# Every second weight load of the experts issued by GpSimd's queue

## The chip, the cores and the metric

The kernel runs on one core of a Trainium2 chip. The metric is the device time of one execution in microseconds. TensorE multiplies, ScalarE and VectorE prepare operands and empty the accumulators, GpSimd does small vector work and can issue DMAs, SyncE only issues DMAs. All DMAs run on the core's 16 DMA engines, whoever issues them.

## What is computed

Four transformer layers on x of shape (1, 256, 1024) in float32: two of a first block, two of a second. The last layer ends in a mixture of eight experts, and this is where the change lies (the rest cut):

```
def swiglu(x, w13, w2):
    a, g = jnp.split(x @ w13, 2, axis=-1)
    return (jax.nn.silu(a) * g) @ w2

def moe_ffn(x, router_w, router_b, w13, w2):
    logits = x @ router_w + router_b
    top_v, top_i = lax.top_k(logits, 2)
    wts = jax.nn.softmax(top_v, axis=-1)
    gate = jnp.einsum('bsk,bske->bse', wts, jax.nn.one_hot(top_i, 8))
    y = jnp.zeros_like(x)
    for e in range(8):
        y = y + gate[..., e:e + 1] * swiglu(x, w13[e], w2[e])
    return y
```

w13 of an expert is 1024 x 7168, w2 is 3584 x 1024. All eight experts' weights, 352 MB, are read once; a layer norm follows.

## The kernel before

**Slots.** All weights lie in memory as a stream of slots, [128 partitions, 2048 words], 1 MB each; this document counts the experts' slots from 0. An expert has 42: 28 for the hidden layer (seven chunks of 512 columns, four slots each) and 14 for the down projection. So the experts have slots 0 to 335. `Stream` plans for each slot where it lands (`place`), which slot held that buffer before (`before`) and which count of the buffer's semaphore tells of its landing (`turn`). From slot 2 on the ring is four buffers used once, then raw0 to raw2 and spare0, spare1 in turn, so that a buffer comes round every five slots.

**What happens to a slot.** Matmuls run as three products of float32 halves. A slot is loaded by `s_slot`, SyncE's DMA at L2595, when the rest of the slot before it in the buffer has been taken (`lo`). ScalarE copies it, in two halves of 1024 columns, to the rounded part wh (L1163, `a_hi`), in one of three sets, for which TensorE must have finished the slot three earlier (`freed`). VectorE takes the rest, wl = raw - wh, also in two halves (L1617, `v_lo`). This read is the last of the raw buffer. TensorE multiplies wh and wl with the tokens (L480 to L482).

**Experts.** Tokens are gathered per expert by products with a selection, 128 at most (GH, GL). After each chunk come an activation (TT, TU), a transpose (L710) and a split (EH, EL). The result of experts 0 to 6 goes to Y (L1172, ScalarE) and from there, by GpSimd's DMA at L2562 in `g_parts`, to a part of scratch_parts in memory. At the end GpSimd issues four indirect DMAs (L2568) that gather each token's rows of the parts into CHOICE[0] to CHOICE[3], once expert 7's last hidden chunk is multiplied. VectorE adds them to X (L2376, `v_add_choice`): its order, written out by hand, puts one addition behind the rest of slot 330, one behind that of 331, of 332 and of 333. Expert 7's own result goes by YH and YL through a product into X (L2330), then the norm and the stores to out.

**Order.** Each engine runs its instructions in the order in which they are written, and a wait holds all behind it. SyncE's queue holds the loads of all slots in order. GpSimd's holds its small vector work up to the last norm but one, then the seven stores and the four gathers, and then the last norm's two roots. The lines for the heavy case (more than 128 tokens for an expert) are compiled and not run here.

Of the kernel before, what the change touches and what calls it, by code (L numbers as in the profile page):

```python
# [243 lines left out]
    return EXPERTS + EXPERT * e  # L244


class Stream:


    def __init__(self):  # L250
        plan = [s for f in (layer_one_slots, layer_two_slots) for l in range(2) for s in f(l)]
        plan += [s for e in range(8) for s in expert_slots(e)]
        self.words = [slot_words(s) for s in plan]
        self.split = [s != "mlstm" for s in plan]
        self.half = [sum(r1 - r0 for _, _, r0, r1, _, _ in s[:1]) // 2 if s != "mlstm" else 0 for s in plan]
        self.source, at = [], 0
        for s, n in enumerate(self.words):
            if s == expert_slot(8):
                at = self.source[expert_slot(0)]
            self.source.append(at)  # L260
            at += 128 * n
        self.number, c = [], 0
        for split in self.split:
            self.number.append(c)
            c += split
        ring = ["raw0", "raw1", "raw2"]
        more, once, spare = ["more0", "more1"], ["once0", "once1", "once2", "once3"], ["spare0", "spare1"]
        into = {BASE[0] + MIX + 3: more, BASE[1] + MIX + 3: more, BASE[2] + BR + 3: more}
        self.place, self.before, self.turn = [], [], []
        held, turns = {}, {}  # L270
        for s in range(len(plan)):
            if s in into:
                ring = more + ring
            if s in (BASE[1] + 2, BASE[2] + 2, BASE[3] + 2):
                ring = [r for r in ring if r not in more]
            if s == EXPERTS + 2:
                ring = once + ring + spare
            r = ring.pop(0)
            if r not in once:
                ring.append(r)  # L280
            self.place.append(r)
            self.before.append(held.get(r))
            turns[r] = turns.get(r, 0) + (s > 0)
            self.turn.append(turns[r])
            held[r] = s


def program(nc, x_d, pos_d, ws_d, vec_d, row_d, ln_d, rel_d, relb_d, rw_d, cst_d, one_d, lnc_d, out_d):
# [6 lines left out]
    stream = Stream()  # L295
    ctx = ExitStack()
    with ctx:
# [134 lines left out]
            signals.append(Signal(ctx.enter_context(nc.semaphore("s_" + name)), step))  # L432
            return signals[-1]

        landed = {n: ctx.enter_context(nc.semaphore("s_" + n)) for n in raws}
        x_in, cst_in, small_in = [signal(f"x{t}_in", 16) for t in range(2)], signal("cst_in", 16), signal("small_in", 16)
        ident_in, zeroed = signal("ident_in", 16), signal("zeroed")
        first_half, second_half = signal("first_half", 16), signal("second_half", 16)
# [712 lines left out]
        def a_hi(s):  # L1151

            while a_at[0] <= min(s, until[0]):
# [2 lines left out]
                if not stream.split[n]:  # L1156
                    continue
                half = stream.words[n] // 2
                A.wait_ge(landed[stream.place[n]], 16 * stream.turn[n])
                if c >= NSET:  # L1160
                    A.wait_ge(*freed[c - NSET])
                for i in range(2):
# [1393 lines left out]

        def g_parts():

            for e in range(7):
                for h in range(2):  # L2560
                    G.wait_ge(*out("dn", ("e", e), 0, h))
                G.q.dma_start(parts[128 * e:128 * e + 128, :], Y[e % 2][:, :]).then_inc(*part_out[e % 2].mark(e))  # L2562
            G.wait_ge(*picked.at())
            for x in (5, 6):
                G.wait_ge(*part_out[x % 2].at(x))
            G.wait_ge(*full("gu", ("e", 7), 6, 0))
            for i in range(4):
                G.q.indirect_dma_start(  # L2568
                    out=CHOICE[i][:, :], out_offset=None, in_=parts,
                    in_offset=bass.IndirectOffsetOnAxis(ap=ROWS[:, i:i + 1], axis=0),  # L2570
                    bounds_check=7 * 128 - 1, oob_is_err=False).then_inc(*choice_in[i].mark())

        def s_slot(n):

# [23 lines left out]
        def sync_front():  # L2598
# [15 lines left out]
            S.q.dma_start(PT[0:32, 384:392], rel_d).then_inc(*small_in.mark())  # L2614
            S.q.dma_start(PT[0:8, 512:896], lnc_d).then_inc(*small_in.mark())
            for n in range(3, expert_slot(8)):
                s_slot(n)
                if n == BASE[1] + HID + 4:
                    S.wait_ge(*scr_out.at())
                    S.wait_ge(*out("sc", 1, "b", 1, 3))  # L2620
# [118 lines left out]
```

## Time and profile before

| | us |
|---|---|
| median of 3 runs | 2260.6 (2260.22 to 2260.81) |
| the profiled execution | 2262.25 |
| its span | 2261.0 |
| TensorE busy in it | 2241.1 (99%) |
| VectorE busy | 1733.3 (77%) |
| ScalarE busy | 1370.5 (61%) |
| GpSimd busy | 83.6 (4%) |

The experts run from about 1290 us to the end. The DMA engines move 568.75 MB for SyncE's queue in all, 5.77 MB for GpSimd's (the software queue, q0) and 9.52 MB for ScalarE's (q10). A SyncE queue's row is written SPq, and L2595 is line 2595 of the kernel. A matmul's recorded duration overlaps the next one's, so TensorE's busy time doesn't show how fast it goes; the steps of the engines that wait for it do.

### The profile page before, as it was taken

What the parts mean: (1) busy time and instruction counts of PE and PEld (TensorE: products, weight loads), DVE (VectorE), ACT (ScalarE), POOL (GpSimd) and SP (SyncE); (2) the same over time, 40 slices, a digit from 0 to 9 for tenths busy, and PEclk for the clock granted to TensorE, in tenths of its full rate; (3) what the DMA queues carried; (4) which work ended last, traced back from release to release, by engine and by line L of the source; (5) the groups of instructions that cost most, each with busy time, mean ns of one, the idle gap of its engine ahead of it and who ended that gap; (6) DMA issues with size and microseconds to landing.
All of it is one profiled execution on the core that took longest, in us unless ns stands there. A gap on an engine that the chain in (4) does not pass through costs nothing.

```text
span 2261.0 us, 30455 instructions
## 1 busy us (share of the span) xinstructions
PE 2241.1 (99%) x12336; PEld 1926.5 (85%) x12336; DVE 1733.3 (77%) x2226; ACT 1370.5 (61%) x1794; POOL 83.6 (4%) x106
## 2 busy tenths in 40 slices
PE   9999999999999999999999999999999999999997
PEld 6998888898888999888899888888888888888886
DVE  6976556877554578655678898989998899989898
ACT  5654444655443454444454587777777777777775
POOL 2200001300000000000100000000000000000001
PEclk9999999999999999999999999999999999999999
DMA  7455453545544435555434599999999999999996
GB/s 260 161 185 193 176 200 145 178 169 214 188 182 149 179 131 210 189 199 189 151 107 170 225 360 383 378 357 376 379 385 362 364 376 389 366 362 374 386 373 245
DMA packets 95891, 586.05 MB, mean 259 GB/s; under 512 B 21968, under 2 KB 23296, under 8 KB 26624
## 3 DMA queue, kind: packets, MB, share of 16 engines
q1 hardware_dynamic: 80496, 568.75, 66.9%
q10 hardware_dynamic: 13664, 9.52, 1.5%
q0 software_dynamic: 1584, 5.77, 0.6%
q8 instruction: 99, 1.62, 0.3%
q14 instruction: 48, 0.39, 0.0%
HBM read 579.27 MB, written 4.73 MB: 258 GB/s over the span
## 4 chain that ended last, share of the span: by engine, by line
PE 95%; DVE 2%; issue 1%; ACT 1%; DMA 1%; POOL 0%; ACTq 0%; DVEq 0%
PE bank L480 28%; PE bank L482 28%; PE bank L481 28%; PE bank L477 9%; PE bank L710 2%; PE bank L756 1%; DVE wl L1617 1%; PE bank L510 1%; DMA raw<-in_ws 1%; POOL SM L2469 0%; PE bank L804 0%; ACT wh L1163 0%; DVE BIAS L1963 0%; DVE X L2330 0%; DVE X L2376 0%
## 5 line engine op out<-in xcount | busy, mean ns | idle before, releaser
L1617 DVE TENSOR_TENSOR wl<-raw,wh 128x1024 fp32r<-128x1024 f32 x698 | 820.1, 1223 | 229.1 <-ACT wh L1163 225.7
L1163 ACT ACTIVATE wh<-raw 128x1024 fp32r<-128x1024 f32 x704 | 704.5, 1054 | 305.5 <-PE bank L482 264.6
L480 PE MATMUL bank<-wh,GH 128*128 128x512 f32 x896 | 352.7, 394 | 0.0
L482 PE MATMUL bank<-wh,GL 128*128 128x512 f32 x896 | 349.3, 390 | 0.0
L481 PE MATMUL bank<-wl,GH 128*128 128x512 f32 x896 | 348.9, 389 | 0.0
L1617 DVE TENSOR_TENSOR wl<-spare,wh 128x1024 fp32r<-128x1024 f32 x264 | 310.0, 1221 | 30.4 <-ACT wh L1163 28.0
L1163 ACT ACTIVATE wh<-spare 128x1024 fp32r<-128x1024 f32 x264 | 264.2, 1054 | 58.9 <-PE bank L482 56.8
L480 PE MATMUL bank<-HH,wh 128*128 128x256 f32 x832 | 239.6, 288 | 0.0
L481 PE MATMUL bank<-HL,wh 128*128 128x256 f32 x832 | 235.3, 283 | 0.0
L482 PE MATMUL bank<-HH,wl 128*128 128x256 f32 x832 | 235.3, 283 | 0.0
L480 PE MATMUL bank<-wh,HH 128*128 128x512 f32 (+1 forms) x600 | 224.9, 375 | 2.5 <-DVE wl L1617 2.3
L482 PE MATMUL bank<-wh,HL 128*128 128x512 f32 (+1 forms) x600 | 223.4, 372 | 0.0
L481 PE MATMUL bank<-wl,HH 128*128 128x512 f32 (+1 forms) x600 | 223.3, 372 | 0.0
L482 PEld LDWEIGHTS bank<-wh,GL 128*128 128x128 f32 x896 | 168.2, 188 | 35.6
L481 PEld LDWEIGHTS bank<-wl,GH 128*128 128x128 f32 x896 | 168.4, 188 | 33.9
L480 PEld LDWEIGHTS bank<-wh,GH 128*128 128x128 f32 x896 | 168.3, 188 | 33.6
L480 PE MATMUL bank<-wh,EH 128*128 128x512 f32 x448 | 176.4, 394 | 0.5 <-DVE wl L1617 0.4
L481 PE MATMUL bank<-wl,EH 128*128 128x512 f32 x448 | 174.7, 390 | 0.0
L482 PE MATMUL bank<-wh,EL 128*128 128x512 f32 x448 | 174.5, 390 | 0.0
L1617 DVE TENSOR_TENSOR wl<-more,wh 128x1024 fp32r<-128x1024 f32 x94 | 111.0, 1222 | 73.0 <-ACT wh L1163 72.8
L480 PEld LDWEIGHTS bank<-HH,wh 128*128 128x128 f32 x832 | 159.3, 192 | 3.5 <-issue 3.0
L481 PEld LDWEIGHTS bank<-HL,wh 128*128 128x128 f32 x832 | 159.5, 192 | 0.2
(295 smaller groups left out, 3420.7 us busy)
## 6 DMA issues: line engine op xcount, KB each, us to landing
raw<-in_ws SPq DMA_DIRECT2D x352, 1024.0 KB, 6.3
spare<-in_ws SPq DMA_DIRECT2D x132, 1024.0 KB, 7.0
more<-in_ws SPq DMA_DIRECT2D x48, 1024.0 KB, 4.8
once<-in_ws SPq DMA_DIRECT2D x4, 1024.0 KB, 12.0
scratch_parts<-Y POOLq DMA_DIRECT2D x7, 512.0 KB, 8.4
REL<-in_relb ACTq DMA_DIRECT2D x4, 768.0 KB, 12.8
LNB<-in_ln ACTq DMA_DIRECT2D x3, 1024.0 KB, 5.8
LNB<-in_ln ACTq DMA_DIRECT2D x4, 512.0 KB, 4.3
```

Of the source, the lines that this page charges most:

```text
L477: return T.q.matmul(o, l, r, start=start, stop=stop)
L480: T.q.matmul(o, l[0], r[0], start=start, stop=False)
L481: T.q.matmul(o, l[0], r[1], start=False, stop=False)
L482: return T.q.matmul(o, l[1], r[0], start=False, stop=stop)
L510: ins = T.q.transpose(room[:, 128 * c:128 * c + 128], src[:, a:a + 128], ident)
L710: ins = T.q.transpose(room[:, 128 * k:128 * k + 128], TU[t][:, 128 * k:128 * k + 128], ident)
L756: ins = T.q.transpose(room[:, 128 * n:128 * n + 128], LB[t][:, 256 * h + 128 * i:256 * h + 128 * i + 128], ident)
L1163: A.q.activation(sets[c % NSET][0][:, half * i:half * i + half], raws[stream.place[n]][:, half * i:half * i + half], ACT.Copy).then_inc(*h ...
L1617: V.q.tensor_tensor(wl[:, half * i:half * i + half], raw[:, half * i:half * i + half], wh[:, half * i:half * i + half].bitcast(f32), ALU.s ...
```

## The change

Slots of odd number from 9 to 335 are issued by GpSimd, through its own DMA queue, in place of SyncE. They keep their buffers, and they wait for the same rest of the slot before. Since the two queues' landings in one buffer can't share a semaphore's count, the landings by GpSimd have semaphores of their own (`lands`), and ScalarE waits for the one that belongs to the slot.

```
+def by_pool(s):
+    return EXPERTS + 8 < s < expert_slot(8) and (s - EXPERTS) % 2 == 1
...
+            own = r + "_pool" if by_pool(s) else r
+            turns[own] = turns.get(own, 0) + (s > 0)
+            self.turn.append(turns[own])
+            self.lands.append(own)
...
-                A.wait_ge(landed[stream.place[n]], 16 * stream.turn[n])
+                A.wait_ge(landed[stream.lands[n]], 16 * stream.turn[n])
...
+            n = expert_slot(0) + 9
             for e in range(7):
+                while n < expert_slot(e + 1) + 6:
+                    g_slot(n)
+                    n += 2
                 for h in range(2):
                     G.wait_ge(*out("dn", ("e", e), 0, h))
                 G.q.dma_start(parts[128 * e:128 * e + 128, :], Y[e % 2][:, :]).then_inc(*part_out[e % 2].mark(e))
+            while n < expert_slot(8):
+                g_slot(n)
+                n += 2
             G.wait_ge(*picked.at())
...
+        def g_slot(n):
+
+            r = stream.place[n]
+            if stream.before[n] is not None:
+                G.wait_ge(*lo.at(stream.before[n], 1))
+            if r.startswith("spare"):
+                G.wait_ge(*full("rt", 1))
+            words = stream.words[n]
+            G.q.dma_start(raws[r][:, 0:words], bass.AP(ws_d.tensor, stream.source[n], [[words, 128], [1, words]])
+                          ).then_inc(landed[stream.lands[n]], 16)
...
             for n in range(3, expert_slot(8)):
-                s_slot(n)
+                if not by_pool(n):
+                    s_slot(n)
```

The GpSimd queue at the end of the program, before: the last two stores of parts and, next to them, the four gathers (L2562 is the store, L2568 the gather).

```order
84 L2562 DMA scratch_parts<-Y_78 128x1024 [waits s_out7,s_out6]
85 L2562 DMA scratch_parts<-Y_77 128x1024 [waits s_out1,s_out0]
86 L2568 DMA CHOICE_79<-scratch_parts,ROWS 128x1024 [waits s_part0_out,s_full5,s_part1_out,s_picked]
87 L2568 DMA CHOICE_80<-scratch_parts,ROWS 128x1024
88 L2568 DMA CHOICE_81<-scratch_parts,ROWS 128x1024
89 L2568 DMA CHOICE_82<-scratch_parts,ROWS 128x1024
```

The same place now (L2594 is `g_slot`, L2581 the gather; the last row of a slot is slot 335 in spare1):

```order
214 L2594 DMA raw<-in_ws 128x2048 [waits s_lo]
215 L2594 DMA spare_87<-in_ws 128x2048 [waits s_lo]
216 L2594 DMA raw<-in_ws 128x2048 [waits s_lo] x2
217 L2594 DMA spare_89<-in_ws 128x2048 [waits s_lo]
218 L2581 DMA CHOICE_79<-scratch_parts,ROWS 128x1024 [waits s_part0_out,s_full5,s_part1_out,s_picked]
219 L2581 DMA CHOICE_80<-scratch_parts,ROWS 128x1024
220 L2581 DMA CHOICE_81<-scratch_parts,ROWS 128x1024
221 L2581 DMA CHOICE_82<-scratch_parts,ROWS 128x1024
```

Between the last store and the first gather there now stand the loads of expert 7 from its slot 7 on, up to slot 335, which waits for the rest of slot 330.

VectorE's order at the end, the same before and after (L1617 takes the rest of a slot, both halves; L2376 adds a gathered tile; row 1403 is slot 330, row 1412 slot 335):

```order
1403 L1617 TENSOR_TENSOR wl<-spare_89,wh 128x1024 [waits s_hi] x2
1404 L2376 SCALAR_TENSOR_TENSOR X<-CHOICE_79,PICK,X 128x1024 [waits s_choice_weight,s_scaled,s_choice0_in]
1405 L1617 TENSOR_TENSOR wl<-raw,wh 128x1024 [waits s_hi] x2
1406 L2376 SCALAR_TENSOR_TENSOR X<-CHOICE_80,PICK,X 128x1024 [waits s_choice1_in]
1407 L1617 TENSOR_TENSOR wl<-raw,wh 128x1024 [waits s_hi] x2
1408 L2376 SCALAR_TENSOR_TENSOR X<-CHOICE_81,PICK,X 128x1024 [waits s_added,s_choice2_in]
1409 L1617 TENSOR_TENSOR wl<-raw,wh 128x1024 [waits s_hi] x2
1410 L2376 SCALAR_TENSOR_TENSOR X<-CHOICE_82,PICK,X 128x1024 [waits s_added,s_choice3_in]
1411 L1617 TENSOR_TENSOR wl<-spare_87,wh 128x1024 [waits s_hi] x2
1412 L1617 TENSOR_TENSOR wl<-spare_89,wh 128x1024 [waits s_hi] x2
```

Nothing moved here; what moved is the gather that row 1404 waits for, behind the load that waits for row 1403.

## Rows read from the trace of the kernel before

**Rows 1.** Windows (busy us of each engine, count, clock, DMA share, GB/s): body of experts.
```profile
1300.00:2205.00 905.00, 905.00 (x4140) 750.46 (x4138) 818.25 (x784) 707.92 (x787) 4.03 (x7) 1.00 0.97 373
```
**Rows 2.** Waits from 1300 to 2200 us (total, times, longest), engines and SyncE's queue.
```profile
ACT wh L1163 <- PE bank L482: 140.8, 212, 1.0
...
SPq L2595 <- DVE wl L1617: 794.0, 314, 13.6
```
**Rows 3.** Landing of the spare slots' 125 DMAs, 1300 to 2200 us.
```profile
DMA to landing us min/median/max: 4.7/7.0/9.2
```
**Rows 4.** Timeline (start, us): SyncE's loads of slots 2 to 5 and 43, ScalarE's split of 43.
```profile
1280.10 2.03 SPq L2595 DMA_DIRECT2D once<-in_ws  x4
...
1397.44 0.33 SPq L2595 DMA_DIRECT2D raw<-in_ws  x1
...
1407.57 2.01 ACT L1163 ACTIVATE wh<-raw 128x1024 fp32r<-128x1024 f32 x2 [0.71 <-PE bank L482]
```
**Rows 5.** Line L1617 (ns min/median/max): 1300 to 2205 us, then 1411.4 to 1416.
```profile
L1617 DVE TENSOR_TENSOR wl<-raw,wh x382: 1215/1219/1228, 1305.7 to 2203.6; 128x1024 fp32r<-128x1024 f32 x191
...
L1617 DVE TENSOR_TENSOR wl<-spare,wh x4: 1219/1222/1227, 1411.8 to 1415.2; 128x1024 fp32r<-128x1024 f32 x4
```
**Rows 6.** Timeline of the end: ScalarE's splits of 328 to 330, VectorE from 330 on.
```profile
2218.69 2.01 ACT L1163 ACTIVATE wh<-raw 128x1024 fp32r<-128x1024 f32 x2 [0.71 <-PE bank L482]
2221.41 2.01 ACT L1163 ACTIVATE wh<-spare 128x1024 fp32r<-128x1024 f32 x2 [0.71 <-PE bank L482]
2224.75 2.01 ACT L1163 ACTIVATE wh<-spare 128x1024 fp32r<-128x1024 f32 x2 [1.33 <-DMA spare<-in_ws]
...
2225.85 2.36 DVE L1617 TENSOR_TENSOR wl<-spare,wh 128x1024 fp32r<-128x1024 f32 x2 [0.98 <-ACT wh L1163]
2228.13 1.28 DVE L2376 SCALAR_TENSOR_TENSOR X<-CHOICE,PICK,X 128x1024 f32<-128x1024 f32 x1
...
2238.73 1.28 DVE L2376 SCALAR_TENSOR_TENSOR X<-CHOICE,PICK,X 128x1024 f32<-128x1024 f32 x1
```
**Rows 7.** Chain that ended last, a piece of it (start, us).
```profile
2231.88 1.06 DVE X L2376
```
**Rows 8.** DMA view: windows 1280.4 to 1281.2, 1411.4 to 1415.7, 1415.7 to 1418.5, 2207.7 to 2212.
```profile
GB/s 0 0 0 0 0 0 0 0 0 0 0 0 0 0 0 0 0 0 0 0 0 0 0 0 0 0 0 0 0 0 0 0 410 0 0 819 819 0 0 0
...
DMA packets 186, 1.39 MB, mean 324 GB/s; under 512 B 16, under 2 KB 16, under 8 KB 16
...
q1 hardware_dynamic: 186, 1.39, 101.0%
...
q0 software_dynamic: 144, 0.52, 45.8%
...
q1 hardware_dynamic: 230, 1.66, 94.7%
```
**Rows 9.** GpSimd's DMAs: timeline of first store, first and last gather; landings of gathers, stores.
```profile
1411.42 0.80 POOL L2562 DMA_DIRECT2D scratch_parts<-Y  x1 [133.23 <-ACT Y L1172]
...
2207.70 1.09 POOL L2568 DMA_INDIRECT CHOICE<-scratch_parts,ROWS  x1 [77.82 <-PE bank L482]
...
2211.70 0.99 POOL L2568 DMA_INDIRECT CHOICE<-scratch_parts,ROWS  x1 [0.30 <-issue]
...
DMA to landing us min/median/max: 8.6/12.7/16.9
...
DMA to landing us min/median/max: 6.7/8.4/9.3
```
**Rows 10.** Windows around the first store, and after the last one's issue.
```profile
1409.90:1412.90 3.00, 3.00 (x15) 2.49 (x14) 2.21 (x2) 2.65 (x4) 0.80 (x1) 1.00 1.04 399
1412.90:1415.90 3.00, 3.00 (x15) 2.48 (x14) 3.00 (x4) 2.19 (x3) 0.00 (x0) 1.00 0.92 279
...
1418.00:1426.00 8.00, 8.00 (x37) 6.64 (x36) 7.64 (x10) 6.51 (x7) 0.00 (x0) 1.00 1.01 424
...
2130.90:2133.90 3.00, 3.00 (x14) 2.47 (x14) 3.00 (x4) 2.20 (x3) 0.00 (x0) 1.00 0.97 255
```

More of the change, by code:

```diff
@@ L268, in __init__ @@
         into = {BASE[0] + MIX + 3: more, BASE[1] + MIX + 3: more, BASE[2] + BR + 3: more}
-        self.place, self.before, self.turn = [], [], []
+        self.place, self.before, self.turn, self.lands = [], [], [], []
         held, turns = {}, {}
@@ L282, in __init__ @@
             self.before.append(held.get(r))
-            turns[r] = turns.get(r, 0) + (s > 0)
-            self.turn.append(turns[r])
+            own = r + "_pool" if by_pool(s) else r
+            turns[own] = turns.get(own, 0) + (s > 0)
+            self.turn.append(turns[own])
+            self.lands.append(own)
             held[r] = s
@@ L433, in signal @@
             return signals[-1]
-        landed = {n: ctx.enter_context(nc.semaphore("s_" + n)) for n in raws}
+        landed = {n: ctx.enter_context(nc.semaphore("s_" + n)) for n in sorted(set(stream.lands))}
         x_in, cst_in, small_in = [signal(f"x{t}_in", 16) for t in range(2)], signal("cst_in", 16), signal("small_in", 16)
```

## The prediction, made before the changed kernel was run

> **What bounds the kernel now.** I read the windowed busy times first. From 1300 to 2205 us, TensorE is busy in all 905 us at a granted clock of 1.00 (the 2.4 GHz level), VectorE in 818 and ScalarE in 708, and the DMA engines move 373 GB/s at a busy share of 0.97 [rows 1]. The waits of that stretch name no engine waiting for a DMA: ScalarE waits 141 us for TensorE to give back a split set, and SyncE's queue waits 794 us for VectorE to free a raw buffer [rows 2]. So in the body of the experts the weights arrive early, the matmuls set the pace, and SyncE spends its time waiting, not issuing: an issue lasts 0.33 us [rows 4]. Nothing is to be won by sharing its issuing.
>
> How early do they arrive? A landing takes 4.7 to 9.2 us, median 7.0 [rows 3]. Slot 43 is issued at 1397.44 and ScalarE begins to split it at 1407.57 [rows 4], 10.1 us later, so 3.1 us lie between the median landing and its use. Behind that stands a second cover. ScalarE may start on a slot when TensorE has finished the one three earlier; two slots of 2.72 us (2218.69 to 2221.41 [rows 6]) then remain, 5.4 us, and the new slot needs about 2.3 (half a split 1.05, half a rest 1.22 [rows 5]). That leaves 3.1 us more: TensorE starves when a landing takes longer than about 13.2 us.
>
> The end is different. From slot 330 on VectorE is the path: rests of slots and four additions of the gathered tiles alternate, and the chain of waits runs through them [rows 6, 7].
>
> **Part 1: SyncE issues 164 slots fewer** (9, 11, ... 335). 164 x 0.33 us lie inside its 794 us of waiting. Slots that stay on SyncE wait for the same rest as before; only the neighbours' places in the queue go. Worth 0.
>
> **Part 2: each of these slots starts later.** A DMA of SyncE on an idle queue shows its first packet 1.0 us after its issue (issued 1280.10, the first bytes fall in the 33rd of 40 slices of the 0.8 us from 1280.4, at 1281.1 [rows 4, 8]). A DMA of GpSimd is slower to begin: the store of a part is issued at 1411.42, there is no packet of the software queue by 1415.7, and all 144 come by 1418.5; the gathers issued from 2207.70 have none by 2212.0 [rows 8, 9]. I take 4.4 us, so 3.4 more than SyncE. A GpSimd slot would land after 8.1 to 12.6 us, median 10.4. The longest is still under 13.2. The two queues share the 16 engines, which adds up to one transfer (1 MB at 424 GB/s [rows 10], 2.5 us) to a landing that meets another; but about 2 us of waiting behind a neighbour are already in the median of 7.0, since an unhindered landing takes 4.7. The lateness doesn't add up either: the slot that follows in the same buffer is five further, so it is SyncE's, with 3 us to spare. I take 0 for the body. The cover that hides it is 3.1 + 3.1 us; if it is gone, the next part's rival B says what it costs.
>
> The Trainium skill (DMA: Bandwidth & Descriptors, Specifications) gives a first byte after about 1 us for GpSimd's path and 0.6 for SyncE's. This trace disagrees for GpSimd (4.4), and I go by the trace.
>
> **Part 3: does VectorE suffer?** At 818 of 905 us it has little to spare, so blocked instructions would matter. The four rests that run from the store's issue at 1411.42 to 1416 take 1219 to 1227 ns, as the 382 rests of slots in raw do over the whole body (1215 to 1228) [rows 5]. 0 us.
>
> **Part 4: GpSimd's own queue.** Two kinds of DMA stand in it. The seven stores of parts are needed only by the gathers and two experts later: free, even if a slot in front holds them. Slot 7 of the next expert stands behind each store, which waits for the Y copy; it waits itself for the rest of a slot that TensorE must first make room for, after expert 0's last product, and the Y copy waits for no more than that product. 0 us.
>
> The four gathers of the end are not free. Before, they are issued from 2207.70, as soon as expert 7's last hidden chunk is multiplied. Now slots up to 335 come first, and 335 waits for the rest of slot 330, which ends at 2225.85 + 2.36 = 2228.2 [rows 6]. On VectorE the first addition stands right behind that rest, and behind the addition the rests of 331 to 335, for which TensorE waits. Step by step:
> - Rest of 330: before, its split waited 1.33 us for a DMA that competed with the gathers [rows 6]. Without them it starts one step of 2.72 after 2221.41, at 2224.1, 0.6 earlier: rest ends 2227.6.
> - Issue of slot 335 (0.5 to 0.8, as of a store [rows 9]) and 0.3 between issues: first gather issued 2228.4.
> - Its landing took 8.6 us before (least of the four [rows 9]): 2237.0. Lower bound 6.7 us, the fastest store of the same size [rows 9]: 2235.1. Upper bound: slot 335's 1 MB is ahead in the same queue, 2.5 us more, 2239.5; and if the four landings spread as before (last issued about 4.0 after the first, landing 16.9 after its issue: 2249.3 against the fourth addition's 2238.73 [rows 6, 9]), +10.6.
> - The first addition ran at 2228.13; now at 2237.0: **+8.9 us**, with +7.0 and +13 as ends (11.4, and the spread on top). From there VectorE's chain repeats in its old steps of 3.5 us, against gathers that come some 3.7 apart, so I add 0.5.
> TensorE can't cover this: it has slots 329 and 330 left, some 5 us, and the five slots after them need VectorE. What follows slot 335 (YH, YL, the scatter, the norm, the stores, 16.5 us) is unchanged and moves along.
>
> **Sum.** The profiled execution took 2262.25 us (span 2261.0), 1.65 above the median of 2260.6. 2262.25 + 0 + 0 + 0 + 9.4 = 2271.6 for it, and **2270.0 us** as a median: 0.4% slower. Own range of this case 2266 to 2275.
>
> **Rival B: the DMA engines become the bound in the body.** In all seven cases the weight stream is slow from 1.5 to 4.5 us after a GpSimd store is issued, before its first packet moves: 279 GB/s at the first and 255 at the last, against 399 in the 3 us ahead of the first and 424 after it [rows 10]. If a weight DMA of GpSimd does this too, it costs 3 x (424 - 279) / 424 = 1.0 us of the engines' time. A pair of slots then needs 2 x 2.47 + 1.03 = 5.97 us. TensorE's pair takes 5.68: 373 GB/s over 905 us less 3.7 MB of stores are 318 slots, 2.84 each. 0.29 x 164 = 47 us, and the tail: **2317 us**, up to 2330 where down-projection pairs (5.44) are not averaged with the others. For it: seven of seven. Against it: the gathers, also GpSimd's, show no such dip (1.66 MB in the 4.3 us from 2207.7, 386 GB/s [rows 8]), so it may belong to stores. It decides from 0.74 us of lost time per DMA on.
>
> **Rival C: landings over 13 us now and then**, where a store lies between two slots (three GpSimd DMAs in 6 us, seven times) or where slots queue in pairs: 1 to 3 us each, 2275 to 2290.
>
> **Rival D, not slower: the gather lands in time.** The 4.4 us may be the cost of waking an idle GpSimd (the first store came after 133 us of idleness [rows 9]) and not of each DMA. If a busy one starts in SyncE's 1.0 us, the first gather has its 0.5 MB by 2228.4 + 1.0 + 1.3 + 0.4 = 2231.1, +3.0 us, 2263.6. It decides below 4.2 us from issue to landing (2232.6, 4.5 us after 2228.13). This is also what the skill's first byte of 1 us, cited above, would make of the tail.
>
> **How the numbers follow.** Tail alone 0.50 (2270); B 0.30 (2295 to 2335); C 0.12; D 0.08, of which 0.02 goes below 2256. The range 2263 to 2320 leaves out the rest of D (about 0.05) and the upper half of B (about 0.13). This kernel's runs can tell about 0.2% (4.5 us) from no change. Faster by more than that 0.02, within it 0.06, slower 0.92.
>
> **What would show it.** Right: in 1300 to 2205 TensorE busy throughout and no wait for a DMA; software-queue landings near 10 us; the gathers issued at about 2228; VectorE idle for some 9 us before the first addition, released by the gather; everything behind it 9 us later. B: TensorE with gaps all through the body, splits waiting for DMAs, a busy share near 1 at less than 373 GB/s. C: such gaps only at the stores. D: gathers that land within 4 us. I would be wrong altogether if the gathers were issued before slot 335, or if VectorE's rests grew beyond 1.23 us.

## The result, and the profile after

The changed kernel takes 2269.61 us (median of 6 runs, 2268.45 to 2271.45), the kernel before 2260.55 beside it (6 runs, 2260.13 to 2261.05). The ratio is 1.0039, 95% interval 1.0029 to 1.005: 9.1 us slower. Its profiled execution took 2268.45 us with a span of 2267.2, 6.2 us more than the one of before (2262.25; span 2261.0); it is the fastest of the six.

The program gained six lines, so each line of before has a higher number now: the splits are L1169, the rests L1623, the additions L2382, the products L486 to L488. GpSimd's stores are L2572, its gathers L2581, its weight loads L2594; SyncE's loads are L2619.

First the page of the changed kernel: the queues (packets, MB, share of the 16 engines' span) and the DMA issues (KB each, median us to landing).

```profile
q1 hardware_dynamic: 56880, 396.78, 47.0%
q0 software_dynamic: 25200, 177.74, 20.2%
...
raw<-in_ws POOLq DMA_DIRECT2D x98, 1024.0 KB, 7.8
spare<-in_ws POOLq DMA_DIRECT2D x66, 1024.0 KB, 7.8
```

So the change does what it says: 98 + 66 = 164 loads go through the software queue, and they land 7.8 us after their issue, not the 10.4 that I had forecast. The same two groups read over the body, 1300 to 2200 us, GpSimd's loads first and SyncE's second, against 4.7/7.0/9.2 in [rows 3]:

```profile
DMA to landing us min/median/max: 4.9/7.8/12.4
...
DMA to landing us min/median/max: 4.8/7.9/10.8
```

Both queues are later by about 0.9 us in the median, SyncE's too, and GpSimd's has the longer tail. Did it cost anything? The windowed busy times of the body (columns as in [rows 1]), and the waits of 1300 to 2200 us (total, times, longest):

```profile
1300.00:2205.00 905.00, 904.98 (x4137) 750.13 (x4136) 817.01 (x784) 707.33 (x787) 89.35 (x166) 1.00 0.96 373
```

```profile
ACT wh L1169 <- PE bank L488: 123.9, 188, 1.0
...
ACT wh L1169 <- DMA raw<-in_ws: 12.7, 10, 2.7
...
ACT wh L1169 <- DMA spare<-in_ws: 7.8, 6, 3.0
```

No: ScalarE now waits 16 times for a weight, 20.5 us in all (14 of the 16 for a load of GpSimd), where the list of before had no such wait, and its wait for TensorE shrinks by 17 us in exchange [rows 2]. TensorE stays busy in 904.98 of 905 us at a granted clock of 1.00. The late landings are absorbed by slack that ScalarE had: of the 315 landings of both queues, 12 took over 10.1 us, the time from issue to use that [rows 4] gave.

The end is where the time went. The timelines of ScalarE, VectorE and GpSimd there (start us, us, then in brackets the idle time before and its releaser), to be laid beside [rows 6, 9]:

```profile
2217.35 2.01 ACT L1169 ACTIVATE wh<-raw 128x1024 fp32r<-128x1024 f32 x2 [0.71 <-PE bank L488]
...
2223.89 2.36 DVE L1623 TENSOR_TENSOR wl<-spare,wh 128x1024 fp32r<-128x1024 f32 x2 [0.36 <-ACT wh L1169]
2234.54 1.28 DVE L2382 SCALAR_TENSOR_TENSOR X<-CHOICE,PICK,X 128x1024 f32<-128x1024 f32 x1 [8.29 <-DMA CHOICE<-scratch_parts,ROWS]
...
2244.94 1.28 DVE L2382 SCALAR_TENSOR_TENSOR X<-CHOICE,PICK,X 128x1024 f32<-128x1024 f32 x1
...
2226.54 0.54 POOL L2594 DMA_DIRECT2D spare<-in_ws  x1 [4.90 <-DVE wl L1623]
2227.50 1.08 POOL L2581 DMA_INDIRECT CHOICE<-scratch_parts,ROWS  x1 [0.42 <-issue]
```

Read from the bottom: slot 335 is issued at 2226.54, after a wait for the rest of slot 330; the first gather follows at 2227.50, and VectorE stands idle for 8.29 us until it has landed at 2234.5. In the waits of 2205 to 2267 us the products appear behind it:

```profile
DVE X L2382 <- DMA CHOICE<-scratch_parts,ROWS: 8.3, 1, 8.3
PEld bank L486 <- DVE wl L1623: 6.8, 2, 6.6
PE bank L486 <- DVE wl L1623: 6.2, 1, 6.2
```

TensorE had no such gap before. One step more is in the windows from 2229 us on:

```profile
2229.00:2232.00 3.00, 1.86 (x9) 1.20 (x7) 0.00 (x0) 2.29 (x4) 2.39 (x3) 1.00 0.96 400
2232.00:2236.00 4.00, 0.00 (x0) 0.00 (x0) 1.46 (x2) 0.95 (x2) 0.48 (x1) 0.85 1.01 412
2236.00:2240.00 4.00, 2.99 (x7) 2.41 (x8) 4.00 (x4) 0.00 (x0) 0.00 (x0) 0.50 0.27 112
2240.00:2245.00 5.00, 5.00 (x20) 4.03 (x20) 5.00 (x6) 2.02 (x3) 0.00 (x0) 0.83 0.00 0
```

TensorE has no product from 2230.9 to 2237.0; its granted clock falls in that time, stands at 0.50, the 1.2 GHz level, from 2236 to 2240, and is back to 1.00 in the window from 2245 us. That costs nothing here, since VectorE sets the pace: from the first addition to the end of the span are 32.7 us (2267.2 - 2234.54), and they were 32.9 before (2261.0 - 2228.13).

The two profiled executions are not at the same place when the end begins: slot 328 is split at 2217.35 here and at 2218.69 there [rows 6]. Measured from that split, the first addition comes after 17.19 us, and came after 9.44: **+7.75 us** for the end in the traces. The lead is older than the body: the first split of the experts' slots already starts at 1290.78 after and at 1292.59 before. It is no sign of the change either: in the five traces of kernels that are the same as the one before up to there, this split starts anywhere from 1291.09 to 1293.06, and in the four with shared loads from 1290.78 to 1292.51. One of the first splits of the body, in spare, starts at 1341.41 in the timeline after and at 1343.07 in the one before. From it to the split of 328 are 875.94 us after and 875.62 before: the body costs **+0.3 us** in this one execution (the run below with the same shared loads in the body has 875.65). 7.75 + 0.32 - 1.66 of lead - 0.21 behind the first addition are the 6.2 us between the two spans.

### The profile page after: what moved, and what is told of

It is laid out like the page before. It is cut to its first block, busy times and chain, and to the rows that moved or that the text cites. A ratio compares the mean times of both kernels' runs of the same rounds, so it can differ in the third digit from the quotient of the medians.

```text
span 2267.2 us, 30455 instructions
## 1 busy us (share of the span) xinstructions
PE 2241.7 (99%) x12336; PEld 1926.1 (85%) x12336; DVE 1731.6 (76%) x2226; ACT 1369.8 (60%) x1794; POOL 172.7 (8%) x270
## 4 chain that ended last, share of the span: by engine, by line
PE 95%; DVE 2%; DMA 1%; issue 1%; ACT 0%; POOL 0%; ACTq 0%; SPq 0%; DVEq 0%; POOLq 0%
PE bank L486 28%; PE bank L488 28%; PE bank L487 28%; PE bank L483 8%; PE bank L716 2%; PE bank L762 1%; DVE wl L1623 1%; PE bank L516 1%; DMA raw<-in_ws 0%; POOL SM L2475 0%; DMA CHOICE<-scratch_parts,ROWS 0%; ACT wh L1169 0%; PE bank L810 0%; ACTq L1358 0%; DVE BIAS L1969 0%
## 5 line engine op out<-in xcount | busy, mean ns | idle before, releaser
L1623 DVE TENSOR_TENSOR wl<-raw,wh 128x1024 fp32r<-128x1024 f32 x698 | 819.8, 1222 | 229.0 <-ACT wh L1169 226.2
L1169 ACT ACTIVATE wh<-raw 128x1024 fp32r<-128x1024 f32 x704 | 704.2, 1053 | 306.9 <-PE bank L488 255.5
L486 PE MATMUL bank<-wh,GH 128*128 128x512 f32 x896 | 352.9, 394 | 0.0
L488 PE MATMUL bank<-wh,GL 128*128 128x512 f32 x896 | 349.3, 390 | 0.0
L1623 DVE TENSOR_TENSOR wl<-spare,wh 128x1024 fp32r<-128x1024 f32 x264 | 309.8, 1220 | 31.9 <-ACT wh L1169 30.5
L1169 ACT ACTIVATE wh<-spare 128x1024 fp32r<-128x1024 f32 x264 | 264.1, 1054 | 69.2 <-PE bank L488 61.3
L486 PE MATMUL bank<-HH,wh 128*128 128x256 f32 x832 | 239.6, 288 | 0.0
L488 PE MATMUL bank<-HH,wl 128*128 128x256 f32 x832 | 235.2, 283 | 0.0
L486 PE MATMUL bank<-wh,HH 128*128 128x512 f32 (+1 forms) x600 | 224.9, 375 | 1.6 <-DVE wl L1623 1.6
L488 PE MATMUL bank<-wh,HL 128*128 128x512 f32 (+1 forms) x600 | 223.4, 372 | 0.0
L488 PEld LDWEIGHTS bank<-wh,GL 128*128 128x128 f32 x896 | 168.2, 188 | 35.6
L486 PEld LDWEIGHTS bank<-wh,GH 128*128 128x128 f32 x896 | 168.3, 188 | 34.3 <-DVE wl L1623 0.4
L486 PE MATMUL bank<-wh,EH 128*128 128x512 f32 x448 | 177.4, 396 | 6.2 <-DVE wl L1623 6.2
L488 PE MATMUL bank<-wh,EL 128*128 128x512 f32 x448 | 175.3, 391 | 0.0
L1623 DVE TENSOR_TENSOR wl<-more,wh 128x1024 fp32r<-128x1024 f32 x94 | 111.0, 1222 | 73.1 <-ACT wh L1169 72.9
L486 PEld LDWEIGHTS bank<-HH,wh 128*128 128x128 f32 x832 | 159.3, 191 | 3.5 <-issue 3.0
## 6 DMA issues: line engine op xcount, KB each, us to landing
once<-in_ws SPq DMA_DIRECT2D x4, 1024.0 KB, 13.2
```

The lines of the kernel that those rows point to most:

```text
L486: T.q.matmul(o, l[0], r[0], start=start, stop=False)
L488: return T.q.matmul(o, l[1], r[0], start=False, stop=stop)
L1169: A.q.activation(sets[c % NSET][0][:, half * i:half * i + half], raws[stream.place[n]][:, half * i:half * i + half], ACT.Copy).then_inc(*h ...
L1623: V.q.tensor_tensor(wl[:, half * i:half * i + half], raw[:, half * i:half * i + half], wh[:, half * i:half * i + half].bitcast(f32), ALU.s ...
```

## The experiments

Four concern the end of the program, two the body, three take one buffer away to see what the body's cover is worth, and the last tries to shorten the end. All were run with the kernel before on the same chip: its medians were 2260.78 (24 runs, for the experiments on the kernel before with waiting gathers, the gathers ahead of the last loads, and GpSimd alone), 2260.91 (27, for the last four slots back on SyncE, ScalarE's stores, and the first two with four buffers) and 2260.93 (15, for the last two). They differ from the kernel before or from the changed one, as the text above each diff says.

### The changed kernel with the last four slots back on SyncE

From the changed kernel; slots 329, 331, 333 and 335 leave GpSimd's queue.

```diff
 def by_pool(s):
-    return EXPERTS + 8 < s < expert_slot(8) and (s - EXPERTS) % 2 == 1
+    return EXPERTS + 8 < s < expert_slot(8) - 8 and (s - EXPERTS) % 2 == 1
...
-            while n < expert_slot(8):
+            while n < expert_slot(8) - 8:
                 g_slot(n)
```

> The changed kernel with slots 329, 331, 333 and 335 given back to SyncE; GpSimd issues the 160 loads 9 to 327 and then the gathers, at their old time. Nothing of the weights is ahead of the gathers on GpSimd's queue, and nothing behind them. Theory (the loss comes from gathers and last loads sharing one queue, in either order): 2260.8 us, within 1.0. Rival (some loss belongs to the loads of the body): 2262 to 2266.

Measured: 2261.32 us (11 runs, 2260.53 to 2262.28), ratio 1.0001 (0.9992 to 1.001). GpSimd's last load, its first gather, and VectorE's first addition in the timelines:

```profile
2205.24 0.54 POOL L2594 DMA_DIRECT2D raw<-in_ws  x1 [4.02 <-DVE wl L1623]
2207.78 1.09 POOL L2581 DMA_INDIRECT CHOICE<-scratch_parts,ROWS  x1 [2.00 <-PE bank L488]
...
2227.90 1.28 DVE L2382 SCALAR_TENSOR_TENSOR X<-CHOICE,PICK,X 128x1024 f32<-128x1024 f32 x1
```

The gathers are issued at the old time again, the addition waits for nothing, and the loss is gone, with 160 of the 164 loads still on GpSimd. Its body has the landings of the changed kernel (8.0 us for SyncE's, 7.9 for GpSimd's) and TensorE busy in all 905.00 us. So the whole measurable loss hangs on the four last loads, and none on the other 160.

### The kernel before with gathers that wait for the rest of slot 330

From the kernel before: the wait of slot 335 is given to the gathers, and no load is moved.

```diff
             G.wait_ge(*full("gu", ("e", 7), 6, 0))
+            G.wait_ge(*lo.at(expert_slot(8) - 6, 1))
             for i in range(4):
```

> The kernel before, all loads by SyncE, but GpSimd waits for the rest of slot 330 before it issues the gathers. Theory: the same wait as in the changed kernel, less the 1.0 us that the issue of slot 335 took there ahead of the gathers: first gather issued about 2227.7, landed 7.0 later, 2268.0 to 2269.0 us. Rival (the loads are the cost): 2260.6.

Measured: 2268.7 us (5 runs, 2267.91 to 2269.71), ratio 1.0036 (1.0022 to 1.005). Gather and addition:

```profile
2227.24 1.09 POOL L2569 DMA_INDIRECT CHOICE<-scratch_parts,ROWS  x1 [98.65 <-DVE wl L1617]
...
2234.27 1.28 DVE L2376 SCALAR_TENSOR_TENSOR X<-CHOICE,PICK,X 128x1024 f32<-128x1024 f32 x1 [7.98 <-DMA CHOICE<-scratch_parts,ROWS]
```

The wait alone, without one weight load on GpSimd, costs 7.9 us. Together with the experiment above this is the cause from both sides: taken out, the loss goes; put in alone, it comes. The four landings take 6.7 to 7.0 us here and 6.6 to 7.0 in the changed kernel: slot 335's load ahead of them in their own queue adds nothing to the landing. Its issue adds less than the 1.0 us that I had expected: the first gather is issued 0.95 us after the end of the rest here (2226.29) and 1.25 us after it in the changed kernel (2226.25).

### The same with the rest of slot 328

```diff
+            G.wait_ge(*lo.at(expert_slot(8) - 8, 1))
             for i in range(4):
```

> As the one before, with the wait two slots (5.4 us) earlier, for the rest of slot 328: a smaller dose of the same delay. Theory: the first gather is issued at about 2222 and lands after 7.0 to 8.6 us (the last weights still compete), so the first addition is 1 to 3 us late: 2261.5 to 2264.5 us. Rival (the loads are the cost): 2260.6. If the delay of the gathers cost more than their lateness on VectorE: over 2265.

Measured: 2265.94 us (10 runs, 2263.53 to 2266.38), ratio 1.0021 (1.0012 to 1.0031), more than the range that I had expected, and over the 2265 that I had named as a sign of a cost beyond VectorE's lateness.

```profile
2222.29 1.59 POOL L2569 DMA_INDIRECT CHOICE<-scratch_parts,ROWS  x1 [93.21 <-DVE wl L1617]
...
2231.93 1.28 DVE L2376 SCALAR_TENSOR_TENSOR X<-CHOICE,PICK,X 128x1024 f32<-128x1024 f32 x1 [5.15 <-DMA CHOICE<-scratch_parts,ROWS]
```

Issued 5 us sooner, the first gather is ready only 2.3 us sooner: 9.6 us from issue to use against 7.0, and the other three land 11.3 to 11.7 us after their issues. When the first gather is issued, 3.7 MB of SyncE's loads are still to move here, 1.8 MB in the run above, and 9.5 MB in the kernel before. So a gather's landing is no constant: 7 us at the tail of the weight stream, and 8.6 to 16.9 within it [rows 9]. For this expectation I had carried the 7 us into the wrong neighbourhood. The lateness still accounts for the time: from the split of slot 328 (2217.88) to the first addition are 14.05 us, 4.6 more than before, and the rest of the span is 0.3 longer, 4.9 in all of the 5.2 between the medians.

### The gathers ahead of the last four loads

From the changed kernel: GpSimd keeps the loads, but the gathers come first.

```diff
-            while n < expert_slot(8):
+            while n < expert_slot(8) - 8:
                 g_slot(n)
                 n += 2
             G.wait_ge(*picked.at())
...
                     bounds_check=7 * 128 - 1, oob_is_err=False).then_inc(*choice_in[i].mark())
+            while n < expert_slot(8):
+                g_slot(n)
+                n += 2
```

> The changed kernel, but GpSimd issues the four gathers before slots 329, 331, 333 and 335, so about where they stood in time before (2207 to 2208 us). All 164 loads stay with GpSimd. Theory (the whole loss is the wait of the first addition for a gather issued too late): back to 2260.6 us, within 1.5, and no idle time of VectorE before the first addition. Rival (loads by GpSimd cost time in the body of the experts, by slower landings or a slowed weight stream): stays at 2269 to 2270.

Measured: 2266.35 us (8 runs, 2265.28 to 2268.47), ratio 1.0026 (1.0016 to 1.0037). My expectation missed, and the rival of 2269 to 2270 with it: the order of the queue was mended, and 5.6 us are still lost, of 9.1. The trace is of the slowest of the eight executions (2268.47). The last gather, slot 329, its split and the rest behind it:

```profile
2211.49 0.99 POOL L2581 DMA_INDIRECT CHOICE<-scratch_parts,ROWS  x1 [0.30 <-issue]
2212.49 0.59 POOL L2597 DMA_DIRECT2D spare<-in_ws  x1
...
2228.93 3.90 ACT L1169 ACTIVATE wh<-spare 128x1024 fp32r<-128x1024 f32 x4 [8.44 <-DMA spare<-in_ws]
...
2230.02 4.63 DVE L1623 TENSOR_TENSOR wl<-spare,wh 128x1024 fp32r<-128x1024 f32 x4 [8.08 <-ACT wh L1169]
```

Slot 329 is issued the moment the last gather is, and lands 16.4 us later, with four slow gathers ahead of it in the one software queue. The split waits 8.4 us for it. The addition now has its data; the weight hasn't. Gathers behind loads or loads behind gathers: in one queue, whichever comes second is late. Of the kernels tried, only the one that leaves the last loads on another queue (above) wins the time back.

### GpSimd alone loads the body

From the kernel before: every slot from 9 to 321 of the experts (313 loads) goes to GpSimd, and the last 14 stay with SyncE.

```diff
+def by_pool(s):
+    return EXPERTS + 8 < s < expert_slot(8) - 14
...
             for n in range(3, expert_slot(8)):
-                s_slot(n)
+                if not by_pool(n):
+                    s_slot(n)
```

> Every slot from 9 to 321 is issued by GpSimd (313 loads, none by SyncE between), the rest by SyncE, and the gathers follow at their old place. Theory (landings of GpSimd's loads are covered by some 6 us, an issue of 0.54 us fits in a slot's 2.72): 2260.6 us, within 1.5. Rival (a slowed weight stream of 1.0 us of DMA time for each GpSimd DMA, as the stores show): 2.47 + 1.03 = 3.50 us a slot against 2.84, 0.66 x 313 = 207 us more, about 2470. Rival (landings near the edge of the cover): 2265 to 2300.

Measured: 2261.35 us, ratio 1.0002 (0.9993 to 1.0012); nine of the ten runs lie between 2260.38 and 2262.93. The tenth took 4548.35; there is no trace of it, and I can't say why. The body's window, and the landings of the 311 loads that GpSimd issues from 1300 to 2200 us:

```profile
1300.00:2205.00 905.00, 905.00 (x4140) 750.43 (x4139) 818.16 (x784) 707.88 (x787) 171.01 (x318) 1.00 0.97 373
```

```profile
DMA to landing us min/median/max: 4.8/7.2/9.1
```

This is the hardest test of rival B: if a GpSimd load took 1.0 us from the stream, 313 of them would cost some 207 us. They cost nothing that these runs can show (the interval ends at 1.0012, 2.7 us). It also corrects the landing: GpSimd alone lands in 7.2 us, SyncE alone in 7.0, and the two of them sharing in 7.9. Most of the 0.9 us in the changed kernel comes from two queues taking turns, not from GpSimd. GpSimd's 171 us of work on 318 DMAs, 0.54 each, beside VectorE's rests left those as long as before (818.16 us for 784 instructions, 818.25 in [rows 1]).

### The stores of the parts issued by ScalarE

From the kernel before: the seven stores leave GpSimd, to see whose the dip of the weight stream is.

```diff
                 a_copy(Y[e % 2][:, 512 * h:512 * h + 512], ("dn", ("e", e), 0, h), 512)
+            for h in range(2):
+                A.wait_ge(*out("dn", ("e", e), 0, h))
+            A.q.dma_start(parts[128 * e:128 * e + 128, :], Y[e % 2][:, :]).then_inc(*part_out[e % 2].mark(e))
...
-            for e in range(7):
-                for h in range(2):
-                    G.wait_ge(*out("dn", ("e", e), 0, h))
-                G.q.dma_start(parts[128 * e:128 * e + 128, :], Y[e % 2][:, :]).then_inc(*part_out[e % 2].mark(e))
```

> The kernel before with the seven stores of parts issued by ScalarE instead of GpSimd. The question is whose the dip of the weight stream is (255 to 304 GB/s from 1.5 to 4.5 us after the issue). If it belongs to GpSimd's way of preparing a DMA: no dip, over 380 GB/s there, and the store's first packet about 1 us after its issue. If it belongs to a store from SBUF to memory, whoever issues it: a dip of the same size, near its packets. Time within 1 us of before in both cases, since the landings have slack.

Measured: 2261.19 us (10 runs, 2260.11 to 2262.5), ratio 1.0001 (0.9992 to 1.001). The windows from 1.5 to 4.5 and 4.5 to 7.5 us after the first store's issue at 1411.4, and from 1.5 us after the last one's:

```profile
1412.90:1415.90 3.00, 3.00 (x15) 2.48 (x14) 3.00 (x3) 2.75 (x3) 0.00 (x0) 1.00 1.01 415
1415.90:1418.90 3.00, 3.00 (x15) 2.47 (x14) 3.00 (x4) 2.01 (x3) 0.00 (x0) 1.00 0.87 311
2130.90:2133.90 3.00, 3.00 (x15) 2.49 (x14) 3.00 (x3) 2.77 (x3) 0.00 (x0) 1.00 0.99 403
```

The dip to 279 and 255 GB/s [rows 10] is gone from its place: 415 and 403. So its place belongs to a store whose DMA GpSimd prepares. But these rates count every queue, and ScalarE's store (queue q10) begins 1.4 to 2.2 us after its issue, so that it fills the window itself. From 1412.9 to 1415.9 the queues moved (packets, MB, share), first in the kernel before and then here:

```profile
q1 hardware_dynamic: 103, 0.83, 91.8%
...
q1 hardware_dynamic: 104, 0.72, 56.9%
q10 hardware_dynamic: 144, 0.52, 44.2%
```

The weights on q1 get no more here than before. Over nine us from the same point, which take in the whole store in both kernels, the windows are, before and here:

```profile
1412.90:1421.90 9.00, 9.00 (x42) 7.44 (x41) 8.28 (x9) 7.25 (x8) 0.00 (x0) 1.00 1.00 380
...
1412.90:1421.90 9.00, 9.00 (x42) 7.44 (x41) 8.74 (x8) 7.53 (x9) 0.00 (x0) 1.00 0.95 343
```

At the last store the same nine us have 367 GB/s before and 370 here, and the body's mean is 373. So GpSimd's store sets when the rate falls, and nothing here shows that it takes more from the weights than ScalarE's does. Such windows also stand where there is no store: the kernel before moves 273 GB/s at a busy share of 0.95 from 1724.5 to 1727.5. What makes the 311 a little later here, no run tells. In the time nothing moves, as before: the body has the slack.

### The kernel before with four buffers instead of five

To learn what stands behind "it costs nothing", one spare buffer is taken away.

```diff
-        more, once, spare = ["more0", "more1"], ["once0", "once1", "once2", "once3"], ["spare0", "spare1"]
+        more, once, spare = ["more0", "more1"], ["once0", "once1", "once2", "once3"], ["spare0"]
```

> The kernel before without the buffer spare1, so that a raw buffer comes round every four slots and a landing may take 10.9 - 3.6 = 7.3 us before its split is late, and 3.1 more before TensorE starves. It measures how thin the cover may get. Landings of 7.0 us still fit: 2260.6 to 2266 us, the loss in single late splits. If the two covers were not what I take them for: over 2280.

Measured: 2264.14 us (10 runs, 2263.35 to 2265.69), ratio 1.0015 (1.0006 to 1.0024). TensorE is still busy in all 905 us, which doesn't say how fast it goes: from the split of slot 9 to that of slot 328 are 908.41 us here (1310.57 to 2218.98) and 907.00 before (1311.69 to 2218.69). ScalarE now waits for weights, in the waits of 1300 to 2200 us:

```profile
ACT wh L1163 <- DMA raw<-in_ws: 32.9, 55, 2.1
...
ACT wh L1163 <- DMA spare<-in_ws: 15.8, 20, 3.6
```

### The shared loads with four buffers

The same edit in the changed kernel with its last four slots on SyncE, so that the end plays no part.

> The kernel with the last four odd slots back on SyncE, and without spare1. Landings of both queues took 7.9 us at the median in the changed kernel, 0.6 over the 7.3 that four buffers leave. Theory (sharing the loads lengthens landings by about 1 us and this is hidden by the fifth buffer alone): slower than the same four buffers with SyncE alone by 5 to 40 us. Rival (sharing costs nothing even without cover): the same as that one, within 2 us.

Measured: 2301.6 us (4 runs, 2298.1 to 2304.34), ratio 1.0184 (1.0168 to 1.0199), 37.5 us more than SyncE alone with four buffers.

```profile
1300.00:2205.00 905.00, 884.61 (x3982) 721.00 (x3981) 779.05 (x754) 679.30 (x757) 85.58 (x159) 1.00 0.95 358
```

```profile
ACT wh L1169 <- DMA raw<-in_ws: 135.1, 112, 3.6
ACT wh L1169 <- DMA spare<-in_ws: 56.4, 46, 4.0
PEld bank L486 <- DVE wl L1623: 26.3, 29, 2.6
```

This is rival B's picture, splits waiting for DMAs and TensorE with gaps, but without its cause: the DMA share falls to 0.95 instead of rising to 1, so the bound lies with the landings and not with full engines. In the window 3982 products are done, where SyncE alone with four buffers does 4138: 156 less, at 905 / 4138 = 0.219 us each, are 34 us, nearly the whole loss. The medians are only 7.4 us (SyncE) and 7.5 (GpSimd), against 7.1 with SyncE alone. What grows is the spread: the longest are 11.4 and 12.6, against 10.2. Only 6 of the 303 landings take over 10.5 us, though, so single long landings can't make up the loss; it is more likely that lateness passes from slot to slot, which no run here follows step by step. One thing more differs from five buffers: with four, a slot and the next one in its buffer are both odd or both even, so each buffer belongs to one queue alone, and a late slot is no longer followed by one of the other queue. No run tells this apart from the sharing.

### GpSimd alone with four buffers

Which part of those 37.5 us is GpSimd's own lateness, and which the sharing? The edit for four buffers, in the kernel in which GpSimd alone loads the body.

> GpSimd alone loads slots 9 to 321 of the experts (as in the run in which it loads all of them with five buffers) and one spare buffer is taken away, so that four are left. It tells apart why the shared loads lost 37.5 us with four buffers (2301.6 against 2264.1 for SyncE alone). Theory one, the interleaving of two queues makes each landing longer (7.4 to 7.5 us there, 7.1 for SyncE alone), and GpSimd as such is not late: GpSimd alone lands in 7.0 to 7.3 us, ScalarE waits for DMAs 50 to 80 us in all from 1300 to 2200 us (48.7 for SyncE alone, 191.5 shared), TensorE loses less than 5 us of the 905, and the time is 2264 to 2272. Theory two, GpSimd's own lateness per load is what four buffers no longer cover: then all slots are late instead of every second one, ScalarE waits for DMAs 200 us or more, TensorE loses 20 us or more, and the time is 2295 to 2340.

Measured: 2273.55 us (4 runs, 2270.93 to 2279.53), ratio 1.0058 (1.0043 to 1.0074).

```profile
1300.00:2205.00 905.00, 898.37 (x4092) 741.09 (x4091) 808.07 (x775) 703.32 (x777) 171.59 (x319) 1.00 0.96 367
```

```profile
ACT wh L1169 <- DMA raw<-in_ws: 123.2, 170, 3.1
...
ACT wh L1169 <- DMA spare<-in_ws: 45.6, 62, 2.8
```

Between the two, and nearer the first theory. With twice as many loads on GpSimd, the loss against SyncE alone is 9.4 us, not 37.5 (46 products less, 10 us); so if the two costs simply add up, about three quarters of the 37.5 come with the sharing (or with the fixed buffers that go with it). From the split of slot 9 to that of 328 the traces have 908.41 us with SyncE alone, 919.36 with GpSimd alone and 942.90 shared, and with five buffers 907.00, 907.01 and 907.02 (the run with the last four slots back on SyncE). But GpSimd's own 0.3 us of lateness is not free once the cover is thin: the time is 1.6 us above the theory's range, TensorE loses 6.6 us of the 905 instead of less than 5, the median landing is 7.4 us instead of 7.0 to 7.3, and the waits of ScalarE for weights are 168.8 us, over twice the 80 allowed.

### The additions earlier, in the kernel before

The end showed VectorE as the bound behind slot 330, so I tried whether the additions do better ahead of it.

```diff
-                    if e == 7 and 6 <= j < 10:
-                        v_add_choice(j - 6)
+                    if e == 7 and j in (3, 5, 6, 7):
+                        v_add_choice((3, 5, 6, 7).index(j))
```

> The kernel before, with the four additions of the gathered tiles put after the rests of slots 327+0, +2, +3 and +4 of the last ten instead of after four of the last rests, so that VectorE, which sets the pace at the end, has 4.8 us of additions less behind slot 330. Theory: TensorE has gaps of about 0.4 us from 2240 to 2245 us and 0.9 from 2245 to 2250 in the kernel before, which is what the additions cost it, so at most 1.1 us is won: 2259.5 to 2260.9, no change that these runs can show for certain. Rival: the gathers, which landed 8.6 to 16.9 us after their issues at 2207.7 to 2211.7 (the last at 2228.6), are not all there for the earlier additions, VectorE waits for them, and the time is 2262 to 2266.

Measured: 2260.11 us (11 runs, 2259.91 to 2261.03), ratio 0.9997 (0.9988 to 1.0006). The first two additions in its timeline, neither of which waits for its gather:

```profile
2218.33 1.28 DVE L2376 SCALAR_TENSOR_TENSOR X<-CHOICE,PICK,X 128x1024 f32<-128x1024 f32 x1
...
2224.07 1.28 DVE L2376 SCALAR_TENSOR_TENSOR X<-CHOICE,PICK,X 128x1024 f32<-128x1024 f32 x1
```

The 0.8 us between the medians are as forecast and too little to be told from nothing. No kernel tried here is faster than the one before by more than that.

## Why the prediction was right, and where its terms were off

**Part 1, SyncE's 164 issues less, 0 us: right.** SyncE's queue waited 794 us before and 848 after.

**Part 2, the body, 0 us: right in its sum, wrong in its price.** I gave each GpSimd load 3.4 us more than SyncE's, from the first packets of a store and of gathers, and reached a median landing of 10.4 us. It was 7.8, and 7.2 with GpSimd alone. The step that failed is "I take 4.4 us": the nearest rows were of other kinds of DMA. In the packet records of the changed kernel, ten loads of GpSimd meet an empty software queue: eight have their first packet 1.23 to 1.53 us after their issue, and two after 3.9 and 4.05. The stores in the same queue need 4.2 to 5.1 and the gathers 3.9 to 4.4. The slower of the two loads is the very first, as the idea of waking an idle GpSimd would have it, but the gathers follow a load by under 1 us and are as slow as ever, so idleness is not the gathers' reason. Nor is VectorE's work: it stood idle from 2226.25 to 2234.54, while the first gather, issued at 2227.50, took 3.9 us to begin. And a store isn't always slow: where GpSimd alone loads the body, a load is issued 0.5 us behind each store, and the seven stores begin after 1.4 to 2.2 us. What decides between the two levels stays open.

My second term, "the two queues share the 16 engines", I had called already contained in the median; it was in fact the larger part, about 0.7 of the 0.9 us. Two of the signs that I had given for being right were not met: the landings were not near 10 us, and ScalarE did wait for DMAs.

The Trainium skill (DMA: Bandwidth & Descriptors, Specifications) gives about 1 us for GpSimd's first byte; I had set the trace against it, and for most plain loads the runs now come near the page (1.23 to 1.53), for gathers and most stores they don't. Its 0.6 us for SyncE's path stands beside 1.0 in this trace.

The cover is what made the sum right in spite of that. The longest landing was 12.4 us, and TensorE lost 0.02 us, so the 13.2 are not contradicted, and not tested at their edge either. One buffer less takes a slot of 2.72 us from the cover, which leaves 10.5: SyncE alone, at most 10.2 us, keeps TensorE busy in 905.00 of 905 us, while the shared queues with landings up to 12.6 leave it idle for 20.4. The direction fits; the size doesn't follow from the cover, since only 6 landings pass 10.5. My "the lateness doesn't add up" rested on the queues taking turns in a buffer, which they do with five and don't with four.

**Part 3, VectorE, 0 us: right**, with 817.01 us in the body for 818.25.

**Part 4, the stores, 0 us: right.** They wait for the Y copies alone, and nobody waits for them.

**Part 4, the gathers, +8.9 us: the mechanism was right in each step, and the size 1.15 us too large in the trace.** On the axis of the trace of before, 1.34 us later than that of after: the rest of 330 was to end at 2227.6 and ended at 2226.25 + 1.34 = 2227.6. The first gather was to be issued at 2228.4 and was at 2228.84, 0.44 later, mostly because slot 335 was issued 0.29 us after the end of the rest, and not at once. Its landing was to take 8.6 us and took 7.0, 1.6 less; I had taken it from a gather in the middle of the weight stream, and did not ask how little of the stream is left at 2228; my lower bound, 6.7, was nearer. 8.9 + 0.44 - 1.6 = 7.74, and 7.75 was measured. The 0.5 for later additions was not needed: the four stand 10.40 us apart from first to last (2234.54 to 2244.94), 10.60 before.

**Of the 9.1 us between the medians, 7.75 are placed in the end and 0.3 in the body.** Both are of one pair of traces, and the 0.3 did not come back in the other traces with shared loads. The kernel before with the one wait added gives 7.9 by its medians, and the shared loads without the end 0.4, within its error. The remaining 1.0 us lies inside the interval of the ratio (6.6 to 11.3 us) and is less than the 2 us or so by which the start of the experts differs between traces of kernels alike up to there; it stays open. By the placed terms alone the median would be 2268.6; that my 2270.0 came within 0.4 us of the measured one owes something to terms that were too large standing in for what stays open.

**Rival B (2317 us, chance 0.30) fell.** The dip does stand at each of the seven stores, but 313 loads by GpSimd left 373 GB/s and a full TensorE. Its price was misread as well: I set 279 GB/s against the 424 right behind it, in which the stream catches up. Over nine us from the start of the dip the engines moved 380 GB/s at the first store and 367 at the last, about the body's mean of 373. I gave the rival 0.30 on seven of seven; the weight against it, that the gathers show no dip, was the better guide. **Rival C** needed landings over 13 us, and the longest was 12.4. **Rival D** needed a gather within 4.2 us, and none came under 6.6.

## What to carry to other kernels

Before moving a DMA to another engine's queue, write down what already stands in that queue and who waits for it: here 160 of 164 moved loads cost nothing, and with the last four of them a gather that VectorE needed was held up. Mending the order inside the one queue mostly exchanged who is late; keep DMAs with near deadlines of different kinds on different queues. And read a landing time with its company: the same gather took 7.0, 9.6 and 8.6 us as the weight stream around it changed, and the price of one store does not hold for a load, nor even for a store in other company. A rate in a short window says little until its neighbours and its other queues are read too.

## What the runs showed of the hardware that I had not expected

**Two queues lengthen each other's landings at an unchanged rate.** At 373 GB/s in each case, 1 MB landed in 7.0 us (median) with SyncE alone, 7.2 with GpSimd alone, and 7.9 (SyncE) and 7.8 (GpSimd) with loads alternating between them. With four buffers the pair cost 37.5 us over SyncE alone and GpSimd alone 9.4; in the pair each buffer then also belongs to one queue, so the 37.5 are not shown to be the sharing's alone. The Trainium skill (Trainium Kernel Development and Optimization, Key Constraints) says that DMAs of different queues interleave on the same 16 engines and that several issuers save only issue time. The runs agree, and add a price that the rule leaves out.

**The engines move less for about 3 us ahead of the first packet of a store that GpSimd prepares, and make up for it:** 279 and 255 GB/s at the first and last store, 415 and 403 in the same windows when ScalarE issues it and the store itself is in the window, but 380 and 367 against 343 and 370 over nine us. No loss to the weights is shown.

**A GpSimd DMA has no single start-up time.** In the changed kernel it was 1.23 to 1.53 us for eight plain loads and 3.9 to 4.05 for two, 4.2 to 5.1 for a store and 3.9 to 4.4 for a gather, the first of them beside an idle VectorE. Where GpSimd alone loads the body, a store took 1.4 to 2.2. No run here shows what decides.
